# Two of seven weight casts moved into the pair that uses them, behind ScalarE's copy of the first product

## The reference, cut to what matters

```python
h2 = rmsnorm(x, w['norm2_g'])
up = h2 @ w['ffn_up']                       # 1024 -> 2 * 2816: gate columns, then upper columns
up_ext = jnp.concatenate([ffn_hist, up], axis=1)
g_ff, u_ff = jnp.split(causal_dwconv(up_ext, w['ffn_conv_w'], w['ffn_conv_b']), 2, axis=-1)
x = x + (jax.nn.silu(g_ff) * u_ff) @ w['ffn_down']
```

## Time and profile before

| | us |
|---|---|
| median of 3 runs (lowest to highest) | 1880.33 (1875.08 to 1884.22) |
| profiled execution, its own time | 1879.7 |
| span of the profiled execution | 1877.7 |
| TensorE busy in the span | 1799.5 (96%) |
| VectorE, ScalarE, GpSimd busy | 1010.0 (54%), 512.9 (27%), 765.2 (41%) |
| pairs 0 to 17 in the span | 1198.1 to 1589.5 |

### The profile page before, as it was taken

How to read it: one execution, slowest core, us unless ns; L and a number is a source line. 1 busy time by engine, 2 the same in 40 slices (tenths; PEclk the granted TensorE clock), 3 DMA queues, 4 the chain that set the end, 5 groups by cost and what they waited for, 6 DMA issues and landing times.

```text
span 1877.7 us, 31728 instructions
## 1 busy us (share of the span) xinstructions
PE 1799.5 (96%) x11890; PEld 1723.8 (92%) x11890; DVE 1010.0 (54%) x1455; ACT 512.9 (27%) x718; POOL 765.2 (41%) x622
## 2 busy tenths in 40 slices
PE   5889999999999999999999999989999999999998
PEld 4888987888999989999999999989999999899997
DVE  4673244416623345222235379956667667766666
ACT  5201033323321122011122032444444444110012
POOL 2323211013223343433333233688888886333330
PEclk9989999999999999999999999999999999999999
DMA  4120221022122222223224331232222225422302
GB/s 129 47 54 23 63 69 46 12 63 68 51 77 69 69 83 80 74 69 84 74 78 112 109 109 46 69 91 80 68 73 85 77 70 204 151 92 91 110 1 93
DMA packets 167650, 146.09 MB, mean 78 GB/s; under 512 B 14598, under 2 KB 150507, under 8 KB 167526
## 3 DMA queue, kind: packets, MB, share of 16 engines
q1 hardware_dynamic: 163468, 130.73, 23.3%
q10 hardware_dynamic: 4092, 14.13, 2.0%
HBM read 111.59 MB, written 33.21 MB: 77 GB/s over the span
## 4 chain that ended last, share of the span: by engine, by line
PE 66%; POOL 12%; DVE 11%; issue 5%; ACT 2%; DMA 1%; POOLq 1%; ACTq 0%; SPq 0%; DVEq 0%
PE ps L2503 13%; PE ps L2506 12%; PE ps L2509 12%; PE ps L2940 5%; POOL w_lo L1233 3%; POOL w_hi L1233 3%; DVE cv L2307 2%; POOL slot L1233 2%; PE ps L3090 2%; PE pt L3090 2%; PE ps L2712 2%; PE ps L3092 2%; PE ps L3091 2%; PE pt L3092 2%; PE pt L3091 2%
## 5 line engine op out<-in xcount | busy, mean ns | idle before, releaser
L1083 POOL TENSOR_TENSOR mark<-eps 128x1 f32<-128x1 f32 x123 | 42.2, 343 | 814.9 <-PE ps L2509 296.3
L2503 PE MATMUL ps<-h_hi,w_hi 128*128 128x352 f32 x1608 | 362.1, 333 | 8.7 <-POOL w_lo L1090 6.3
L2506 PE MATMUL ps<-h_lo,w_hi 128*128 128x352 f32 x1608 | 348.3, 325 | 0.0
L2509 PE MATMUL ps<-h_hi,w_lo 128*128 128x352 f32 x1608 | 347.9, 324 | 0.0
L2503 PEld LDWEIGHTS ps<-h_hi,w_hi 128*128 128x128 f32 x1608 | 269.6, 190 | 19.8 <-issue 9.4
L2509 PEld LDWEIGHTS ps<-h_hi,w_lo 128*128 128x128 f32 x1608 | 276.8, 189 | 0.0
L2506 PEld LDWEIGHTS ps<-h_lo,w_hi 128*128 128x128 f32 x1608 | 275.6, 189 | 0.0
L1090 POOL TENSOR_TENSOR w_lo<-w_raw,w_hi 128x1024 fp32r<-128x1024 f32 x69 | 179.7, 2605 | 5.5
L2307 DVE SCALAR_TENSOR_TENSOR cv<-ext,pv,cv 128x1072 f32<-128x1072 f32 x88 | 158.2, 1798 | 9.4 <-DVE fstate L2305 1.8
L2427 DVE TENSOR_TENSOR x_acc<-x_acc,ps 128x352 f32<-128x352 f32 (+3 forms) x136 | 70.5, 518 | 42.5 <-PE ps L3092 38.2
L2427 DVE TENSOR_TENSOR x_acc<-x_acc,pt 128x352 f32<-128x352 f32 (+2 forms) x128 | 67.1, 524 | 47.9 <-PE pt L3092 45.1
(11 more groups left out here) (449 smaller groups left out, 3938.8 us busy)
## 6 DMA issues: line engine op xcount, KB each, us to landing
w_raw<-in_w_in SPq DMA_DIRECT2D x52, 512.0 KB, 4.1
w_raw<-in_ffn_up SPq DMA_DIRECT2D x26, 512.0 KB, 4.7
act_in<-act_dram SPq DMA_DIRECT2D x11, 1056.0 KB, 5.1
act_dram<-cv SPq DMA_DIRECT2D x22, 512.0 KB, 2.7
y_all<-in_ffn_up SPq DMA_DIRECT2D x18, 512.0 KB, 4.6
gates_dram<-y_all ACTq DMA_DIRECT2D x16, 528.0 KB, 2.7
cst<-gates_dram SPq DMA_DIRECT2D x16, 528.0 KB, 3.6
w_raw<-in_ffn_down SPq DMA_DIRECT2D x12, 512.0 KB, 4.1
```

Source lines behind the costliest of these rows:

```text
L2503: mm(dst[:, c, 0:CH], f_hi[n][:, k, :], h_hi[:, k, tok], start=k == 0, stop=False)
L2506: mm(dst[:, c, 0:CH], f_hi[n][:, k, :], h_lo[:, k, tok], start=False, stop=False)
L2509: last = mm(dst[:, c, 0:CH], f_lo[n][:, k, :], h_hi[:, k, tok], start=False, stop=k == KD - 1)
```

## The change

The order of ScalarE's list changes, and nothing else. From pair 2 on, c5 and c6 of a pair are no longer made in the pair before but in the pair itself: c5 behind left_save, c6 behind first_tap of the gate column. The next pair's c0 follows c6; c1, c2 and c3 follow first_half_out; c4 follows first_tap of the upper column, and ends the list. In pair 1, the list is as before up to c4 of pair 2. The hardware loop now begins at pair 4; pairs 2 and 3 are unrolled.

```diff
-        def st_pair(q, nxt=None):
+        def st_pair(q, nxt=None, late=0, then=0):
...
-            second = isinstance(i, int) and pair_of(q) == 1
-            if nxt is not None and not second:
-                cast(nxt, raw, 0)
-            first_tap(pair_of(q, NPL - 1), 0, None, (u_read, of(q, 5, 0)), of(q, 2, 2 * NPL - 2))
-            if second:
+            prev = pair_of(q, NPL - 1)
+            if late == 0:
+                if nxt is not None:
+                    cast(nxt, raw, 0)
+            elif late == 2:
+                cast(q, s, 5)
+            first_tap(prev, 0, None, (u_read, of(q, 5, 0)), of(q, 2, 2 * NPL - 2))
+            if late == 4:
                 for n in range(3, 6):
                     cast(q, s, n)
+            elif late > 0:
+                cast(q, s, 6)
+                if nxt is not None:
+                    cast(nxt, raw, 0)
...
             first_half_out(q, of(q, 2, 2 * NPL))
...
+            elif late > 0 and nxt is not None:
+                for n in range(1, 4):
+                    cast(nxt, raw, n)
+                done = 4
...
             first_tap(e, 1, None, (u_read, of(q, 5, 4)), of(q, 2, 2 * NPL - 1))
             if nxt is not None:
-                for n in range(3 if second else 6, 7):
+                for n in range(done, 7 - then):
                     cast(nxt, raw, n)
...
         st_pair((0, 0), (0, 1))
+        st_pair((0, 1), (1, 0), 4, 2)
         od.peel()
-        st_pair((0, 1), (1, 0))
-        with act.Fori(1, NST // 2 - 1) as i:
-            od.enter(i, 1, [(s_cast, 14)], times=2)
-            st_pair((i, 0), (i, 1))
-            st_pair((i, 1), (i + 1, 0))
-        od.leave(NST // 2 - 2)
-        st_pair((NST // 2 - 1, 0), (NST // 2 - 1, 1))
-        st_pair((NST // 2 - 1, 1))
+        st_pair((1, 0), (1, 1), 2, 2)
+        st_pair((1, 1), (2, 0), 2, 2)
+        with act.Fori(2, NST // 2 - 1) as i:
+            od.enter(i, 2)
+            st_pair((i, 0), (i, 1), 2, 2)
+            st_pair((i, 1), (i + 1, 0), 2, 2)
+        od.leave(NST // 2 - 3)
+        st_pair((NST // 2 - 1, 0), (NST // 2 - 1, 1), 2, 2)
+        st_pair((NST // 2 - 1, 1), None, 2)
```

More of the change, by code:

```diff
@@ L1727, in st_pair @@
             first_half_out(q, of(q, 2, 2 * NPL))
-            if second:
+            done = 6
+            if late == 4:
                 cast(q, s, 6)
@@ L1731, in st_pair @@
                     cast(nxt, raw, n)
+                done = 3
+            elif late > 0 and nxt is not None:
+                for n in range(1, 4):
+                    cast(nxt, raw, n)
+                done = 4
             elif nxt is not None:
```

## The result

The changed kernel took 1903.87 us (median of 4, 1899.1 to 1909.26) against 1882.05 for the kernel before in the same series: a ratio of 1.0123, 95% interval 1.0084 to 1.0162. It is slower, by some 22 us; 1898 was forecast. Its profiled execution took 1899.1 us.

The account below looks back on a forecast made before the run. GpSimd paced the later pairs, and ScalarE's late copy stalled pair 2. Against 1879.7 us: -6.75 at pair 2, +1.15 pair 3, +22.3 pairs 4 to 15, +1.0 pair 16, 0 pair 17, together +17.7, so 1898; range 1874 to 1908.

Parts of the forecast that it names:

- The stall at pair 2: Pair 2: TensorE's wait for left_save falls from 6.8 to 0.9 us, clock stays up; pair 3 starts 6.75 us earlier.
- the sum: All pairs' gains and losses added to the profiled 1879.7 us: together +17.7, giving 1898 us.
- The ring in the loop: Pairs 4 to 15: the cycle from one s3's end to the next, closed on GpSimd, grows from 20.95 to 22.8 us.
- The walk: Step-by-step placing of a pair's operations from the end of s3, by traced durations and gaps: 22.8 us in the loop.
- Taking turns: VectorE's taps and GpSimd's operations exclude each other for whole instructions; r4, r5, r6, s1, s2 take 2.1 us, r0 to r2 1.3.
- Where TensorE waits: In each loop pair TensorE waits 1.6 us for VectorE's part_out before the fourth product and 0.6 before the last.
- Outside the loop: Unrolled pairs with shorter ScalarE gaps: pairs 3 and 16 take 21.7 us (+1.15, +1.0), pair 17 unchanged from 22.47.
- The faster one: Rival: the loop's ring stays hidden, TensorE runs at 20.55 us a pair, 1869 us; chance 0.13.
- the second rival: Nothing to see: one or two of five turns vanish, ring of 20.7 to 22.1 us, 1880 for 21.4; chance 0.16.
- the third: Worse: r4 goes before VectorE's tap, loop pairs of 24 us, 1912 us; chance 0.05.

Follow-up runs that it names:

- experiment 2: The changed kernel with c4 moved ahead of ScalarE's tap of the upper column: 1916.62 us, ratio 1.022 to the kernel before.
- experiment 4: The changed kernel with VectorE's part_out ahead of second_half_out of the pair before, using a second buffer: 1922.55 us, ratio 1.0245 to the kernel before.
- experiment 6: The changed kernel with GpSimd's s3 and s4 each made one place earlier: 1881.50 us, ratio 1.0021 to the kernel before.
- experiment 9: The changed kernel with c4 ahead of the upper tap and c6 ahead of the gate tap: 1901.96 us, ratio 1.0129 to the kernel before.
- experiment 10: The kernel before with c6 alone made in its own pair, behind left_save and the gate tap, c0 following: 1924.06 us, ratio 1.0243.
- experiment 3: The changed kernel without VectorE's second and third tap in pairs 1 to 17 (output differs): 1861.95 us, ratio 0.9921 to the kernel before.
- experiment 5: The kernel before with GpSimd's s3 and s4 each made one place earlier: 1871.84 us, ratio 0.9971.
- experiment 8: The kernel before with c6 directly behind left_save, and GpSimd's s3 and s4 each one place earlier: 1871.49 us, ratio 0.9967.

## Why the prediction was right

*The stall at pair 2.* Right in place: 0.7 us left there (0.9 forecast), the clock up. The pair's 22.34 (22.25 forecast) is partly luck: TensorE's two waits came to 1.2 us and not 1.7, and its busy time to 21.11 and not 20.55. The loop's pairs have that longer busy time too (253.83 / 12 = 21.15); no term of the sum for pair 2 had it. What it was worth was read rightly too, in the sum: pair 3 begins at the ring's pace at once.

*The ring in the loop.* Right in its mechanism, and to 0.3 us in its size: 23.11 a pair for 22.8, or 277.32 for 273.6. The walk had two gaps too short. The gate tap follows second_half_out by 0.26 us (1409.74 to 1410.00) where I had 0.05; and at each second pair VectorE has a pause of its own loop, 0.40, in front of second_half_out, which I left out. The ring from the end of s3 to the next takes 22.99 from 1401.70, and 23.29 in the pair after it, with that pause. Taps and end of second_half_out on VectorE, in the place of the earlier trace rows, and then that pause, one pair later:

```profile
1404.90 1.33 DVE L2322 SCALAR_TENSOR_TENSOR cv<-ext,pv,cv 128x1072 f32<-128x1072 f32 x1 [0.15 <-DVE fstate L2320]
...
1409.55 0.19 DVE L2397 TENSOR_TENSOR ext<-pt,cst 128x32 f32<-128x32 f32 x1
...
1431.91 0.43 DVE L2395 TENSOR_TENSOR ext<-pt,cst 128x264 f32<-128x264 f32 x1 [0.40 <-DVE cv L2322]
```

The walk also gave the ring of kernels that had not run: 23.6 for experiment 2 (24.0 measured), 23.9 for 4 (23.8), 21.4 and 0.3 for 6 (21.65), 22.9 for 9 (22.8), 24.1 for 10 (24.7). The times that were expected from it missed by more: 1916.6 us for 1910 (2), 1922.6 for 1914 (4), 1924.1 for 1916 (10). In 2 and 10 most of that is the 0.4 and 0.6 of the twelve loop pairs; in 4 it lies ahead of them, as pair 4 begins at 1295.3 there and at 1284.8 in the changed kernel.

One reading of the prediction was wrong without harm. It took r3 and r4 of the earlier trace rows as operations beside VectorE's PSUM work, but VectorE stood idle from 1397.15 to 1400.67, through all of r4. s3 (1394.88, 1.30) is the row that shows it, and r0 to r2 did take 1.28 to 1.30 (1419.06 to 1423.25).

*Which step of it costs.* The prediction wrote 1.4 us of each pair to the tap in front of c4. That holds for r4's start (3.61 after s3), but not as a cost that stands alone: experiment 2 took it away from r4, it turned up at r5, and the pair got longer. What lengthens the pair is that both taps have come into the ring: s3, c3, upper tap, VectorE's two taps, second_half_out, gate tap, c6, r6. In the kernel before, GpSimd's operations followed each other and the taps ran beside them; with c6 alone moved behind the gate tap there, the pair grew by 3.8 us (experiment 10). The summary by line of the chain of waits over 1300 to 1540 shows it, first before and then after the change:

```profile
by line: issue 24.5%; POOL w_lo L1233 15.8%; POOL w_hi L1233 15.1%; POOL s_tmp L1263 10.4%; POOL slot L1233 9.6%; POOL s_tmp L1253 6.0%; POOL s_tmp L1258 6.0%; POOL s_tmp L1252 5.9%; DVE cv L2307 1.7%; POOLq L151 1.7%; POOLq L1232 1.0%; ACT
```

```profile
by line: issue 25.0%; DVE cv L2322 11.7%; POOL w_lo L1233 7.0%; POOL s_tmp L1253 6.8%; POOL slot L1233 6.3%; POOL s_tmp L1252 6.3%; POOL s_tmp L1258 5.9%; POOL w_hi L1233 4.4%; ACT cv L1620 4.3%; POOL s_tmp L1263 3.2%; PE pt L3075 2.1%; DVE
```

VectorE's tap goes from 1.7% to 11.7%, and ScalarE's tap comes in with 4.3%.

*Taking turns.* The forms were as forecast: r4, r5, r6, s1 and s2 long (2.09, 2.11, 2.04, 1.81, 2.31), s4 and r0 to r2 short. Experiment 3 shows that the long form goes when VectorE's taps go (r4 and r6 above; r5, s1 and s2 have means of 1.28 to 1.30 there). By the Trainium skill (SBUF — State Buffer, Who interferes with whom), the two exclude each other for the whole instruction. The trace agrees: r4, begun at 1405.31, ends at 1407.40, 1.17 after VectorE's tap of 1404.90 to 1406.23.

*Where TensorE waits.* Right: 1.4 to 1.5 us for part_out and about 0.5 for second_half_out. The working called these waits the effect of the ring, and experiments 4 and 6 show it for part_out.

*Outside the loop.* Pairs 3, 16 and 17 were set too short: 22.38 for 21.7, 23.87 for 21.7, and 23.20 where I wrote no change from 22.47. In all, pairs 2 to 17 grew by 25.0 us for 17.7 forecast: 3.7 of the 7.3 are the loop's. In the unrolled pairs VectorE and GpSimd kept gaps that the walk had taken away with ScalarE's (0.14 for 0.04 between VectorE's taps in pair 3). Pair 16 isn't all unrolled: the upper tap at its start is still made by the loop's last turn, with the loop's gaps (0.22 and 0.33 at 1564.43 and 1564.98), and r4 waits 1.58 as in the loop, where it waits 0.95 in pair 3.

*The rivals.* The faster one would have needed pairs of TensorE's own 20.55, which only came when the ring itself was made shorter (experiments 3, 5 and 8, at 20.56 to 20.60). No turn vanished, as the second rival needed, and r4 didn't come before the tap, as the third did.

## What to carry to other kernels

Before moving an instruction out of the way of a wait, find the ring that sets the pace, and ask what stands in front of the moved instruction in its new place: here the copy was freed, and the taps came into the ring. A stall at the head of a loop that is paced by another engine isn't a gain to be had; it moves on, unless the ring is made shorter. The engine that a wait names may only be following: change it alone and see if the period moves.

## What the runs showed of the hardware that I had not expected

TensorE's clock bore the new short waits. The changed kernel's TensorE waits up to 1.5 us in each loop pair, and the granted clock of the stretch is 1.00. In experiment 2 the longest waits are 2.6 us; its loop has a clock of 0.98, and 0.65 in the 4 us from 1297, part at 1.2 and part at 2.4 GHz, behind a wait of 2.2 us that ended at 1295.65:

```profile
PE ps L3075 <- DVE cst L2387: 25.8, 12, 2.6
```

```profile
1297.00:1301.00 4.00, 4.00 (x24) 4.00 (x24) 3.73 (x3) 1.24 (x3) 3.81 (x2) 0.65 0.05 12
```

The length of a wait doesn't decide it alone. In four stretches of 24 us of that run (from 1284, 1331, 1379 and 1427), each with one wait of 2.2 to 2.6 us, the clock is 0.93. In the four from 1475 on, with waits of 2.2 to 2.6 us too, it is 1.00. In experiment 10, with waits of up to 3.9 us, the loop's clock was 0.94.

And ScalarE's steps stand further apart in the loop than outside it: history copy and tap follow what precedes them by 0.22 and 0.33 us there, by 0.03 to 0.04 in the unrolled pairs. In a ring of waits these gaps count like work. That they are the working out of the awaited values in registers is my reading; no run parts it from other causes.
